# Head sums by a full block of ones, with root and reciprocal on every channel, and odd values by four whole blocks

## The reference, cut to what matters

```python
kk = heads(k * p["k_k"])
kk = kk * lax.rsqrt(jnp.maximum(jnp.sum(kk * kk, -1, keepdims=True), 1e-12))
...
mu = y.mean(-1, keepdims=True)
var = jnp.square(y - mu).mean(-1, keepdims=True)
y = ((y - mu) * lax.rsqrt(var + GN_EPS)).reshape(B, T, D_A) * p["lnx_g"] + p["lnx_b"]
```

## Time and profile before

| | us |
|---|---|
| median of three runs (3231.96 to 3235.2) | 3234.43 |
| the profiled execution | 3232.57 |
| its span, first to last instruction | 3230.8 |
| TensorE busy in the span | 2862.1 (89%) |
| VectorE busy | 1160.0 (36%) |
| ScalarE busy | 607.4 (19%) |
| mean granted TensorE clock, share of full | 0.954 |

### The profile page before, as it was taken

How to read it: one execution, slowest core, us unless ns; L and a number is a source line. 1 busy time by engine, 2 the same in 40 slices (tenths; PEclk the granted TensorE clock), 3 DMA queues, 4 the chain that set the end, 5 groups by cost and what they waited for, 6 DMA issues and landing times. The chain is left out here.

```text
span 3230.8 us, 70364 instructions
## 1 busy us (share of the span) xinstructions
PE 2862.1 (89%) x31462; PEld 1573.5 (49%) x31462; DVE 1160.0 (36%) x2601; ACT 607.4 (19%) x1328; POOL 257.4 (8%) x294
## 2 busy tenths in 40 slices
PE   4799999999988999977988988998987996899987
PEld 2467677767764444443333432432424444455543
DVE  2245554555553762153022022112104435233332
ACT  1223333232321100000000000000002453022230
POOL 1111211121110000001000000000000121010000
PEclk8899999999999999988999999999998997899988
DMA  4100000000005871335999999999992111132202
GB/s 168 38 24 12 25 25 19 12 25 25 4 31 183 294 265 67 117 143 249 429 431 431 430 430 430 430 431 430 430 403 66 41 42 50 33 74 59 58 17 85
DMA packets 192367, 561.75 MB, mean 174 GB/s; under 512 B 32476, under 2 KB 120050, under 8 KB 167510
## 3 DMA queue, kind: packets, MB, share of 16 engines
q1 hardware_dynamic: 192054, 557.45, 43.9%
q10 hardware_dynamic: 32, 0.03, 0.0%
HBM read 554.84 MB, written 2.27 MB: 172 GB/s over the span
## 5 line engine op out<-in xcount | busy, mean ns | idle before, releaser
L2160 PE MATMUL bank<-ex_ring,xe 128*64 128x512 f32 x864 | 337.4, 624 | 35.3 <-DMA mixer_w<-in_exp_w_dram 12.4
L2160 PE MATMUL bank<-mixer_w,xe 128*64 128x512 f32 x576 | 204.1, 626 | 20.9 <-DMA mixer_w<-in_exp_w_dram 10.5
L715 PE MATMUL bank<-hT,first_chunk 128*128 128x512 f32 x384 | 191.2, 624 | 5.6 <-DVE vj L1528 2.9
L2160 PEld LDWEIGHTS bank<-ex_ring,xe 128*64 128x64 f32 x864 | 103.6, 143 | 165.0 <-issue 160.2
L3123 PE MATMUL bank<-h2T_mixer,mixer_w 128*128 128x512 f32 x384 | 176.9, 609 | 2.7 <-PEq L78 2.7
L2160 PE MATMUL bank<-ex_ring,hidT 128*64 128x512 f32 x448 | 170.7, 598 | 2.1 <-DMA h2T_mixer<-in_exp_w_dram 2.0
L2703 PE MATMUL bank<-h2T_mixer,mixer_w 128*128 128x512 f32 x320 | 146.5, 607 | 12.9 <-ACT mixT L2801 8.1
L2160 PE MATMUL bank<-h2T_mixer,xe 128*64 128x512 f32 x304 | 142.7, 625 | 17.0 <-DMA mixT<-in_exp_w_dram 16.1
L2160 PE MATMUL bank<-mixT,xe 128*64 128x512 f32 x304 | 142.2, 623 | 10.6 <-DMA ex_ring<-in_exp_w_dram 9.8
L1467 DVE TENSOR_TENSOR pm<-bank,m_level 128x512 f32<-128x512 f32 x120 | 82.8, 690 | 172.0 <-PE bank L812 171.5
L2374 DVE TENSOR_TENSOR x<-x,bank 128x512 f32<-128x512 f32 x64 | 43.7, 686 | 245.4 <-PE bank L2198 245.4
(11 more groups left out here) (511 smaller groups left out, 5541.6 us busy)
## 6 DMA issues: line engine op xcount, KB each, us to landing
ex_ring<-in_exp_w_dram SPq DMA_DIRECT2D x82, 2048.0 KB, 22.2
mixer_w<-in_exp_w_dram SPq DMA_DIRECT2D x54, 2048.0 KB, 22.5
h2T_mixer<-in_exp_w_dram SPq DMA_DIRECT2D x28, 2048.0 KB, 22.0
mixT<-in_exp_w_dram SPq DMA_DIRECT2D x28, 2048.0 KB, 22.6
ws_w<-in_ada_w_dram SPq DMA_DIRECT2D x40, 1024.0 KB, 5.2
mixer_w<-in_odd_w_in_dram SPq DMA_DIRECT2D x32, 512.0 KB, 3.9
first_chunk<-in_w_in_dram SPq DMA_DIRECT2D x24, 512.0 KB, 3.9
mixer_w<-in_even_w_in_dram SPq DMA_DIRECT2D x24, 512.0 KB, 4.1
```

The costliest lines, as they stand in the source:

```text
L715: last = mm(PROJ[:], wj[:, c, i, :], hT[:, c, 0:T], start=(c == 0), stop=(c == KT - 1))
L2160: r[e] = mm(out[a, :], lhs[j][:, a], w[:, j, 512 * c:512 * c + 512], start=(first and j == 0), stop=(last and j == len(lhs) - 1), skip_gro ...
```

## The change

Key lengths: `squares` is now two matmuls of `sqj` (512 and 256 columns) with the block `head_ones` (128 by 128, ones within a head) as weights, so every channel of a head gets the sum, in place. `clamp` is two VectorE instructions of 512 and 256 columns, `root` one ScalarE instruction of 768. `unit_k` moves from (2,0) to (1,4), x = 0, and there takes the reciprocal of 768 columns and then multiplies from SBUF. `invert`, `widen` and `spread_inverse` go. Deviations: `variance` is one matmul of 512 columns, `deviation` a root of 512 columns, and `normed` starts with a reciprocal of 512 columns; `inverse_deviation`, `widen_rstd` and `spread_rstd` go. Scratch takes in a turn: two for the key sums, where there were one and two, and none for the deviations' way back. Odd mixer: GpSimd first copies the two outer strips of `hT` side by side into `outer`, and the values take four matmuls of 128 rows per `t`.

```diff
@@ -720,22 +719,9 @@
                 pe.wait_ge(S["sq_done"], j + 1)
-                o = sc.take(pe, "ks", j)
-                for t in range(NT):
-                    for g in range(0, P, 32):
-                        last = mm(o[g:g + 32, 2 * t:2 * t + 2], sqj[:, t * P + g:t * P + g + 32], k.head_ones[:, ::HEAD],
-                                  start=True, stop=True, skip_group_check=True)
-                sc.fill(last, "ks", j)
-
-            def spread_inverse(j):
-                if not live(j):
-                    return
-                pe.wait_ge(S["inverse_wide"], j + 1)
-                for i in range(2):
-                    o = sc.take(pe, "inverse", j, i)
-                    for t in range(4 * i, min(4 * i + 4, NT)):
-                        last = mm(o[:, (t - 4 * i) * P:(t - 4 * i + 1) * P], sqj[:, t * P:t * P + P], k.ident[:], start=True, stop=True)
-                    sc.fill(last, "inverse", j, i)
+                for i, c in enumerate(HALVES):
+                    o = sc.take(pe, "ks", j, i)
+                    sc.fill(mm(o[:, 0:c.stop - c.start], k.head_ones[:], sqj[:, c], start=True, stop=True), "ks", j, i)
 
@@ -1010,20 +996,7 @@
                 o = sc.take(pe, "var", j)
-                for t in range(NX):
-                    for g in range(0, P, 32):
-                        last = mm(o[g:g + 32, 2 * t:2 * t + 2], ysq[:, t * P + g:t * P + g + 32], k.head_ones[:, ::HEAD],
-                                  start=True, stop=True, skip_group_check=True)
-                sc.fill(last, "var", j)
-
-            def spread_rstd(j):
-                if not live(j):
-                    return
-                pe.wait_ge(S["rstd_wide"], j + 1)
-                o = sc.take(pe, "rstd", j)
-                for t in range(NX):
-                    last = mm(o[:, t * P:t * P + P], ysq[:, t * P:t * P + P], k.ident[:], start=True, stop=True)
-                sc.fill(last, "rstd", j)
+                sc.fill(mm(o[:], k.head_ones[:], ysq[:], start=True, stop=True), "var", j)
 
@@ -1065,7 +1038,6 @@
                     project(b, K_V, 2)
-                    spread_rstd(a)
                 if at == (1, 1, 1):
@@ -1079,7 +1051,6 @@
                     project(b, R_X, 3)
-                    spread_inverse(b)
                 if at == (2, 0, 1):
@@ -1262,14 +1233,9 @@
                 if live(j):
-                    sc.settled(act, "ks", j)
-                    f(length[:], length[:], ACT.Sqrt).then_inc(S["ss_root"], 1)
-
-            def widen(j):
-                if live(j):
-                    act.wait_ge(S["ss_inv"], j + 1)
-                    f(sqj.rearrange("p (n c) -> p n c", c=HEAD), length[:].rearrange("p t h -> p (t h)").unsqueeze(2).to_broadcast([P, 2 * NT, HEAD]),
-                      ACT.Copy).then_inc(S["inverse_wide"], 1)
+                    sc.settled(act, "ks", j, 0)
+                    sc.settled(act, "ks", j, 1)
+                    f(sqj, sqj, ACT.Sqrt).then_inc(S["ss_root"], 1)
 
@@ -1308,9 +1274,7 @@
                         act.wait_ge(S["zeroed"], 1)
-                    if j:
-                        act.wait_ge(S["rstd_wide"], j)
-                    sc.free(f(rstd[:], z[:, 0:2 * NX], ACT.Sqrt, scale=1.0 / HEAD, bias=eps[:, 0:1]), "var", j)
+                    sc.free(f(ysq[:], z[:], ACT.Sqrt, scale=1.0 / HEAD, bias=eps[:, 0:1]), "var", j)
 
@@ -1335,8 +1299,6 @@
                     deviation(a)
-                if at == (1, 0, 1):
-                    widen_rstd(a)
                 if at == (1, 1, 0):
@@ -1352,7 +1314,6 @@
                     x0(j, 2)
-                    widen(b)
                 if at == (2, 0, 0):
@@ -1371,12 +1332,6 @@
                     x0(b, 0)
-
-            def widen_rstd(j):
-                if live(j):
-                    act.wait_ge(S["rstd_done"], j + 1)
-                    f(ysq[:].rearrange("p (n c) -> p n c", c=HEAD), rstd[:].unsqueeze(2).to_broadcast([P, 2 * NX, HEAD]),
-                      ACT.Copy).then_inc(S["rstd_wide"], 1)
 
@@ -1559,26 +1514,21 @@
                 if live(j):
-                    z = sc.read(dve, "ks", j)
-                    sc.free(ts(length[:].rearrange("p t h -> p (t h)"), z[:, 0:2 * NT], 1e-12, None, ALU.max), "ks", j)
-
-            def invert(j):
-                if live(j):
-                    dve.wait_ge(S["ss_root"], j + 1)
-                    dve.reciprocal(length[:], length[:]).then_inc(S["ss_inv"], 1)
+                    for i, c in enumerate(HALVES):
+                        z = sc.read(dve, "ks", j, i)
+                        sc.free(ts(sqj[:, c], z[:, 0:c.stop - c.start], 1e-12, None, ALU.max), "ks", j, i)
 
             def unit_k(j):
                 if not live(j):
                     return
-                for i, c in ((0, slice(0, 512)), (1, slice(512, TA))):
-                    z = sc.read(dve, "inverse", j, i)
-                    sc.free(stt(kkj[:, c], kj[:, c], col(j, 9), z[:, 0:c.stop - c.start], ALU.mult, ALU.mult), "inverse", j, i)
+                dve.wait_ge(S["ss_root"], j + 1)
+                own.last(dve.reciprocal(sqj, sqj))
+                stt(kkj[:], kj[:], col(j, 9), sqj, ALU.mult, ALU.mult).then_inc(S["unit_made"], 1)
 
             def rate_times_kk(j):
                 if not live(j):
                     return
-                sc.settled(dve, "inverse", j, 0)
-                sc.settled(dve, "inverse", j, 1)
+                dve.wait_ge(S["unit_made"], j + 1)
                 dve.wait_ge(S["t1_done"], j + 1)
@@ -1615,18 +1565,13 @@
 
-            def inverse_deviation(j):
-                if live(j):
-                    sc.settled(dve, "var", j)
-                    dve.reciprocal(rstd[:], rstd[:]).then_inc(S["rstd_done"], 1)
-
             def normed(j):
                 if not live(j):
                     return
                 sc.settled(dve, "center", j)
-                z = sc.read(dve, "rstd", j)
-                sc.free(tt(yj[:], yj[:], z[:], ALU.mult), "rstd", j)
-                sc.settled(dve, "rstd", j)
+                sc.settled(dve, "var", j)
+                own.last(dve.reciprocal(ysq[:], ysq[:]))
+                own.last(tt(yj[:], yj[:], ysq[:], ALU.mult))
                 sc.settled(dve, "bonus", j)
@@ -1646,8 +1591,6 @@
                     shift(b, K_X)
-                if at == (1, 0, 0):
-                    inverse_deviation(a)
                 if at == (1, 1, 1):
@@ -1656,8 +1599,6 @@
                 if at == (1, 4, 0):
-                    invert(b)
-                if at == (2, 0, 1):
                     unit_k(b)
@@ -3024,6 +2965,7 @@
         masked = k.sb("na_masked", [P, 2, 2, 3, SPAN * ROWS], s)
+        outer = k.sb("na_outer", [P, KT, 2, KEY_BLOCK], s)
         q = k.sb("na_q", [P, 2, T], s)
@@ -3063,6 +3005,7 @@
             own = Steps(pool, own_p)
+            pool.tensor_copy(outer[:], hT[:].rearrange("p j (b c) -> p j b c", c=KEY_BLOCK)[:, :, ::T // KEY_BLOCK - 1, :]).then_inc(S["outer_made"], 1)
             pool.memset(table[:], 0.0).then_inc(S["zeroed"], 1)
@@ -3109,16 +3052,15 @@
                         pe.wait_ge(S["qk_moved"], 1 + j * 2 + i - 1)
+                    if i == 2 and isinstance(j, int) and j == 0:
+                        pe.wait_ge(S["outer_made"], 1 + 1)
                 for t in range(4 * half, 4 * half + 4):
                     if i == 2:
-                        for edge in range(2):
-                            at = edge * (T - KEY_BLOCK)
-                            mm(o[rows_of(edge), 0:P], hT[:, t, at:at + KEY_BLOCK], w[:, i, t, :],
-                               start=(t == 0), stop=(t == KT - 1), skip_group_check=True)
-                        for n in range(1, NX):
+                        for n in range(NX):
                             at = (2 * n - 1) * KEY_BLOCK
-                            last = mm(o[:, n * P:n * P + P], hT[:, t, at:at + P], w[:, i, t, :],
-                                      start=False, stop=(t == KT - 1), skip_group_check=True)
+                            tokens = hT[:, t, at:at + P] if n else outer[:, t].rearrange("p b c -> p (b c)")
+                            last = mm(o[:, n * P:n * P + P], tokens, w[:, i, t, :],
+                                      start=(t == 0 and n == 0), stop=(t == KT - 1), skip_group_check=True)
                     else:
                         last = mm(o[:], w[:, i, t, :], hT[:, t, :], start=(t == 0), stop=(t == KT - 1))
                 if half:
```

9 lines of the change are left out of this document (4 added, 5 removed).

## The result

The changed kernel takes **3259.8 us**, the median of 4 runs (3259.11 to 3261.34), against 3234.81 for the kernel before on the same chip. The ratio is 1.0077, 95% interval 1.006 to 1.0094. The profiled execution took 3259.61 us, span 3257.9, mean granted clock 0.946 (0.954 before).

The account below looks back on a forecast made before the run. TensorE was taken to bound scan and odd mixer, VectorE counting only where TensorE waits. Scan +35.5, odd mixer -20 and clock +9.8 gave +25.3 on 3232.57; with the median 1.9 above that execution, 3260 us, range 3241 to 3279.

Parts of the forecast that it names:

- The price of a wide reciprocal: VectorE, extended from rows of 4 to 12 columns at 6.25 ns an element: 3.35 us for 512, 4.95 for 768.
- Second place: (1,3) to (2,1): the 768-wide reciprocal delays the update; the product of (2,0) starts 6.2 us later, TensorE idles 3.3.
- First place: (1,1) and (1,2): the 512-wide reciprocal delays the mask; the product of (1,3) starts 2.0 us later instead of 0.6 earlier.
- A full turn: One full turn of the scan ends 4.4 us later, without the clock; six such turns give 26.4.
- Opening and turn 0: Start of the scan: opening pass +2 us (between 0 and 5), turn 0 +2.4 with only the keys' stall.
- The clock: TensorE's clock falls to 1.2 GHz behind the new stalls: one fall of 1.4 us in each of seven turns, +9.8.
- The scan: All turns and the opening pass together: +35.5 us before the clock's +9.8.
- three conditions for being wrong: Reciprocal of 768 under 3.5 us, TensorE's wait at (2,0) under 2 us, or scan growth under 20 us.
- The odd mixer: Values projection 2.5 us shorter for each of eight pairs, all on TensorE: -20 us, bounds 17 and 22.
- The clock did not hold: Rival: stalls come but busy stretches around them keep 2.4 GHz: +15.5, 3250 us; chance 0.22.
- fall at both places in every turn: Rival: thirteen clock falls of 1.4 us, +18 in place of +9.8: 3268 to 3276 us; chance 0.14.
- a cheap reciprocal: Rival: wide reciprocals cost less per element; 3225 us at 3.8 ns, near 3202 at a plain product's price; chance 0.08.

Follow-up runs that it names:

- keys-only kernel: The change without the deviations' part (wide key lengths and new odd mixer, deviations as before): 3239.2 us, ratio 1.0016 to the kernel before.
- filled kernel: The whole change plus added TensorE products of 512 columns inside its stalls at (1,2) and (1,4): 3254.7 us, ratio 1.0041 to the kernel before.
- deviations-only kernel: The change without the keys' part (wide deviations and new odd mixer, key lengths as before): 3249.35 us, ratio 1.0038 to the kernel before.

## Why the prediction was right, and where it was off

The forecast was 3260, the result 3259.8. The mechanism was the one forecast; that the number is so near is luck, since several terms missed by 1 to 2 us, in both directions.

- *The price of a wide reciprocal.* 3.35 and 4.95 were taken, 3.35 and 4.94 measured. The line through 4, 8 and 12 columns held over 756 more. The Trainium skill's repeat count of 8 (VectorE: DVE Perf Modes, First, the fixed hardware budget), read as eight cycles an element, does not: from 512 to 768 columns it is (4942 - 3346) / 256 = 6.2 ns.
- *Second place.* A wait of 3.3 at (2,0) was forecast, 3.21 is there, in seven turns. The keys-only kernel, 25 or 19 us for 7 turns and the opening, lies within its expectation.
- *First place.* The price held, and so did the two bits of idle of about 2 us each that the clock's paragraph names, if they are read in turns without a fall: 2.01 + 1.54 in place of 1.37, so 2.2 more. The sum has 2.6 (2.0 later in place of 0.6 earlier). It puts all of this before the product of (1,3), but the larger part, 2.01, comes one step earlier, at the correction of (1,2), which waits for the mask that the reciprocal delays.
- *A full turn*, +4.4 without the clock. Turns without a fall: 110.4, the mean of two, against 105.7, the mean of four, so +4.7.
- *Opening and turn 0.* The first mark comes 5.9 later, of which 2.7 are the reciprocal's 3.35 less the 0.64 by which the correction came earlier, and the first projection began 1.5 earlier in this execution: 4.7, for 2 + 2.4.
- *The clock*, +9.8 as one fall of 1.4 in each of seven turns. This was the weakest step: the sum is about right, the pattern is not. The falls do not come once a turn: two turns have none, others two or more, 63 us more at half clock in all. Their price is some 13 to 16 us in turns 1 to 6 by the filled kernel's table, or 10 to 12 by its whole time, from which 6 us are gone that this kernel loses ahead of them. Part of the time at half clock lies under VectorE's chain and costs nothing, as behind the first stall of turn 2, where the next product starts no later than in turn 1.
- *The scan* was to lose 35.5 + 9.8 = 45.3 up to the odd mixer, and lost 45.2. None of the three conditions for being wrong was met: the reciprocal of 768 took 4.94, the wait at (2,0) is 3.21, the scan grew by far more than 20.
- *The odd mixer*, -20: 18.1 in the profiled execution, and 20 and 14 by the ratios of its two runs alone. A projection is 2.64 shorter, more than the 2.5 taken, but eight times 2.64 is 21 and not all of it arrives. The bounds 17 and 22 held the 18.1 and the 20; the 14 lies below them, with an interval of 9 to 18.
- *The rivals.* The clock did not hold (3250), nor did it fall at both places in every turn (3268 to 3276). That a cheap reciprocal would give 3202 was worked out as the limit; with 0.55 us in its place the kernel took 3210.

The scan's loss of 45 us, for work on TensorE that by the forecast is 0.9 us a turn shorter, has two causes that the experiments separate: the place of two long instructions, and the clock behind it, whose share is known only roughly. Neither is VectorE's load, which rises from 51 to 58 us in 100.

## What to carry to other kernels

Moving a small computation to all channels saves the ways back but multiplies an instruction that costs by the column; price it by the slope of the rows there are, and then look between which two instructions of the other engine's chain it would stand. An engine that is busy half the time still has no gap for one long instruction: cut it to the gaps, or give it to the engine that has one, before giving the idea up. Undo the halves of a change separately, since here one of them was worth 0.4 to 0.6% by itself and was hidden by the other.

## What was not expected

- A TENSOR_SCALAR over 768 columns took 550 ns, but the plain product of the same width 1050. The rows chosen from the trace before did not suggest that the form with one tensor operand costs half, though that trace has it, in its groups:

```profile
L2504 DVE TENSOR_SCALAR rms_xn<-x,rms_ss 128x1024 f32<-128x1024 f32 x4 | 2.7, 748 | 0.0
```

- One and the same product of 768 took 1.02, 1.72 or 2.22 us by its place. So an instruction that is moved must be priced again at its new place, beside what the other engines do there.
- The granted clock fell behind an idle of 1.47 us in the deviations-only kernel, and did not fall behind stalls of 3.2 us in two turns of the change. The length of an idle alone does not tell it.
- The runs of one kernel spread by up to 22 us in the deviations-only kernel (3233 to 3255) and by 14 in the filled one (3250 to 3264), which has no fall left in five full turns. The kernel before spreads as much, 3224 to 3243 on one chip and 3232 to 3256 on another. So the falls of the new stalls are not what makes the spread, and the 2 us of the change (3259.1 to 3261.3) are those of four runs only.
